# A fused two-block transformer in fp32: the first half of the mixer worked tile by tile, the zero stores moved to the last half block

## The chip, the cores and the metric

One core of a Trainium2 chip runs the whole program. The metric is the device time of one execution in microseconds (us), the median of the runs. The core has TensorE (PE in the rows; its weight loads are PEld), VectorE (DVE), ScalarE (ACT), GpSimd (POOL) and SyncE (SP); SP, ACT and POOL also issue DMA transfers, which run on the core's 16 DMA engines.

## The reference

512 tokens of width 1024, all float32. A first block of two layers, then a second block. What matters here is layer 0:

```python
mod = c_act @ ada_w[l] + ada_b[l]                  # 6 vectors of 1024: sh1, sc1, g1, sh2, sc2, g2
hn = modulate(rms_norm(h, norm_mix_g[l]), sh1, sc1)
mix = hgrn2_mixer(hn, ...)                         # q, f, v, g projections, scan over chunks of 16 tokens, w_out
h = h + g1[:, None, :] * mix
hn = modulate(rms_norm(h, norm_ffn_g[l]), sh2, sc2)
h = h + g2[:, None, :] * peer_ffn(hn, ...)
...
def peer_ffn(xn, w_q, subkeys, u, v):
    qr = xt @ w_q                                  # queries
    sc = einsum('thpd,hpnd->thpn', qr, subkeys)    # scores against 128 sub-keys, 4 heads x 2
    ...                                            # top 16 of each, top 16 of their sums: 64 experts a token
    hid = einsum('cd,ced->ce', xc, take(u, ec))    # 64 gathered rows of u for each token
    w = gc * gelu(hid)
    return einsum('ce,ced->cd', w, take(v, ec))    # and 64 of v
```

The scan carries its state from one tile of 128 tokens to the next. The second block has a short convolution, window attention and, at its end, 32 routed experts, whose tokens are scattered into a buffer in HBM of 3264 rows, cleared to zeros beforehand.

## The kernel before, in words

Four tiles of 128 tokens make two halves of 256 (`hf` 0 and 1). Layer 0 of half 0 is `first_pe`, `first_act` and `first_dve`, one Python generator for each engine, whose pieces between two `yield`s ("segments", counted by `s`) are laid out in step. The engines run their own instruction streams and wait on semaphores: `a_pe`, `a_act` and `a_dve` count finished steps by the names in `A_PE`, `A_ACT` and `A_DVE`.

**The order of the program.** Half 0 of the mixer runs alone. Then come four windows of two gathered tiles each (`rows_*`, `w` 0 to 3): POOL gathers rows of u and v, each gather 128 rows of 4 KB, into a ring of six pairs (regions `r2`, `r4`, `r3`); DVE makes the dot products with the u rows (`dots_dve`), PE sums the v rows (`sum_pe`), and the next half block of the network is laid between these steps. Window 0 holds half 1 of the mixer, window 3 half 0 of the second block. Half 1 of the second block runs alone behind the windows, and then the experts.

**Tail of half 0.** Behind the four projections and four levels of masked scores, PE does for both tiles together: the scan (L822 transposes, L831/L834 output, L840 new state), the head norms' sums (L849), the output projection (L188, four groups, each of one tile and 512 columns), the turning of the normed rows (L757), the query projection (L188 over 256 tokens), the turning of the keys (L1062), and the scores (L1069). ACT copies all scores (`sc3`), and only then does `route_dve` pick the experts of tile 0 (L369 to L429, about ten segments), after which POOL issues the first gather (L447).

**Modulation chunks.** The 28 chunks of `CHUNKS` are each 1024 x 512 of `ada_w` or `kv_ada_w`, 2 MB. Chunks 0 to 3 make sh1 and sc1 of layer 0, without which no projection begins. `mod_load` loads a chunk into `r5` or `r6` by turns; a chunk is multiplied with c either by PE (`mod_parts_pe` L667, then a copy L648 on DVE) where `BY_PE` says so, or by DVE (`mod_acc_dve` L651/L653, eight passes). `mod_sum_pe` (L678 or L681) adds over partitions, `mod_out_dve` (L693 to L706) finishes it. `MOD_SEG` says before which segment of half 0 this happens. SP issues chunks 0 and 1 and then the first two blocks of mixer weights; POOL (`mods_pool`) issues each later chunk j once chunk j-2 is done.

**Weights.** SP streams all weights through two slots (`stream`, `load_weights`): block i may be loaded when block i-2 has had its last use (`slot_free`, `A_LAST_USE`).

**Zero stores.** At the end of `mods_pool`, ahead of its first gather, POOL issues 26 stores of zeros (`zero_slots`) from `HOLE` into the experts' buffer `x_slots`.

## Time and profile before

| what | value |
|---|---|
| time of three runs | 3090.72, 3091.57, 3102.13 us; median 3091.57 |
| the profiled execution | 3102.22 us, span 3100.7 us, mean granted clock of TensorE 0.825 |
| busy, of the span | PE 71%, DVE 48%, ACT 15%, POOL 36% |
| moved by DMA | 992.03 MB, mean 320 GB/s |
| chain that ended last | PE 44%, DVE 15%, DMA 14%, issue 9%, POOL 4%, ACT 4% |
| half 0 of the mixer alone | 0 to 323.8 us (its last score matmul) |
| routing of tile 0 | 325.9 to 353.7 us |
| windows of gathers | 354 to 2206 us |
| half 1 of the second block | 2206 to about 2450 us, then the experts |

Busy shares are averages over these stages, which have different limits; a stage is read by what it waits for last. The profiled execution lies 10.65 us above the median, so a sum made on its rows is carried over as a share or a difference. In the rows a matmul in float32 counts as two instructions, and "x16" in a row of the PE are eight matmuls.

### The profile page before, as it was taken

Reading aid. Unit: us, or ns where it says so; the run is one execution under the profiler, and the core shown is the slowest. Engines: PE = TensorE matmul, PEld = TensorE weight load, DVE = VectorE, ACT = ScalarE, POOL = GpSimd, SP = SyncE. Lnnn points to the kernel's source line nnn. Section 1 sums busy time; section 2 is a strip of 40 time slices with the busy share of each in tenths; the row PEclk is TensorE's granted clock in tenths of the full one; section 3 lists DMA queues with packets and bytes.
Section 4 is the critical chain, followed back from the end, with each engine's and each line's share of the span. In section 5 each row is a group of like instructions: output and inputs, shape, how many; then the busy total and the mean of one; then the engine's idle time right before and its main releaser. Section 6 shows DMA issues by size and latency. Waiting matters only on the chain.

```text
span 3100.7 us, 28191 instructions
## 1 busy us (share of the span) xinstructions
PE 2191.7 (71%) x10377; PEld 1247.3 (40%) x10377; DVE 1491.4 (48%) x3207; ACT 470.5 (15%) x790; POOL 1126.9 (36%) x1278
## 2 busy tenths in 40 slices
PE   5998294786547596457886358568797588888873
PEld 3574273533325342325642136233576333232321
DVE  3867699644773425853425865661145212121112
ACT  1212111020102410102510101110222101010111
POOL 2111445565652655642555754455100111010001
PEclk8999697898768797658997678789898789898997
DMA  8984999899996999986999989989433579999994
GB/s 302 345 326 174 360 353 394 335 375 379 337 406 242 359 368 368 341 340 242 320 377 358 371 333 330 319 294 380 153 132 126 212 281 356 391 361 402 390 400 163
DMA packets 269877, 992.03 MB, mean 320 GB/s; under 512 B 26925, under 2 KB 33173, under 8 KB 257463
## 3 DMA queue, kind: packets, MB, share of 16 engines
q0 software_dynamic: 175056, 634.01, 54.2%
q1 hardware_dynamic: 89440, 350.26, 29.8%
q10 hardware_dynamic: 5256, 6.05, 0.6%
q8 instruction: 83, 1.36, 0.2%
q14 instruction: 42, 0.34, 0.0%
HBM read 961.62 MB, written 28.61 MB: 319 GB/s over the span
## 4 chain that ended last, share of the span: by engine, by line
PE 44%; DVE 15%; DMA 14%; another core or an unknown queue 9%; issue 9%; POOL 4%; ACT 4%; POOLq 0%; SPq 0%; DVEq 0%; ACTq 0%
PE psum L188 24%; DMA arena<-in_w_down_dram 7%; PE psum L2089 6%; POOL arena L447 4%; DVE arena L459 4%; PE psum L552 4%; PE psum L2103 3%; DMA arena<-in_peer_v_dram,arena 3%; DMA arena<-in_ada_w_dram 2%; DVE arena L1632 1%; PE psum L1412 1%; PE psum L1188 1%; DVE arena L653 1%; DMA arena<-in_hgrn_w_in_dram 1%
## 5 line engine op out<-in xcount | busy, mean ns | idle before, releaser
L188 PE MATMUL psum<-arena 128*128 128x256 f32 (+4 forms) x3656 | 1015.1, 435 | 175.1 <-issue 122.8
L188 PEld LDWEIGHTS psum<-arena 128*128 128x128 f32 x3656 | 710.9, 200 | 495.7 <-issue 373.2
L447 POOL DMA_INDIRECT arena<-in_peer_u_dram,arena x512 | 489.2, 955 | 475.1 <-DVE arena L459 221.9
L447 POOL DMA_INDIRECT arena<-in_peer_v_dram,arena x512 | 497.7, 972 | 393.0 <-PE psum L552 147.2
L459 DVE CUSTOM_DVE_ANT_0 arena<-arena,psum 128x1024 f32<-128x1024 f32 x512 | 592.6, 1216 | 75.0 <-DMA arena<-in_peer_u_dram,arena 51.6
L552 PE MATMUL psum<-arena 128*32 128x512 f32 x2048 | 327.7, 762 | 185.2 <-DMA arena<-in_peer_v_dram,arena 161.4
L2089 PE MATMUL psum<-arena 128*64 128x512 f32 x1088 | 268.8, 651 | 61.8 <-DMA arena<-in_w_down_dram 60.4
L552 PEld LDWEIGHTS psum<-arena 128*32 128x32 f32 x2048 | 69.1, 126 | 378.9 <-issue 377.1
L2136 DVE TENSOR_TENSOR arena<-arena,psum 64x512 f32<-64x512 f32 x34 | 23.5, 692 | 326.4 <-ACT arena L2117 326.4
L2089 PEld LDWEIGHTS psum<-arena 128*64 128x64 f32 x1088 | 82.9, 150 | 222.0 <-issue 220.0
L2150 POOL DMA_DIRECT2D arena<-x_slots x37 | 19.2, 519 | 397.7 <-DVE arena L2124 379.6
L2103 PE MATMUL psum<-arena 128*64 128x512 f32 x544 | 145.3, 683 | 17.6 <-DVE arena L2140 17.6
L2025 POOL DMA_INDIRECT x_slots<-arena x8 | 7.8, 972 | 274.2 <-DVEq L174 272.0
L653 DVE SCALAR_TENSOR_TENSOR arena<-arena 128x512 f32<-128x512 f32 x133 | 100.0, 752 | 4.7
L2117 ACT ACTIVATE arena<-psum 64x512 f32<-64x512 f32 x34 | 20.0, 589 | 510.2 <-PE psum L2089 510.2
L1632 DVE SCALAR_TENSOR_TENSOR arena<-arena 128x256 f32<-128x256 f32 x240 | 97.3, 479 | 0.0
L757 PE MATMUL psum<-arena 128*128 128x128 f32 x128 | 26.9, 397 | 98.1 <-DVE arena L948 55.6
L1188 PE MATMUL psum<-arena 128*128 128x256 f32 (+1 forms) x208 | 55.2, 434 | 52.1 <-DVE arena L1279 51.3
L2144 DVE COPY arena<-psum 128x512 f32<-128x512 f32 x34 | 23.5, 692 | 127.7 <-PE psum L2103 127.7
L2166 POOL DMA_DIRECT2D x_slots<-arena x68 | 36.9, 542 | 129.0 <-DVE arena L2144 127.5
L599 POOL DMA_DIRECT2D arena<-in_ada_w_dram x22 | 20.4, 929 | 168.2 <-DVE arena L653 97.7
L2103 PEld LDWEIGHTS psum<-arena 128*64 128x64 f32 x544 | 40.9, 156 | 96.6 <-issue 74.4
(328 smaller groups left out, 2011.4 us busy)
## 6 DMA issues: line engine op xcount, KB each, us to landing
arena<-in_w_gate_dram SPq DMA_DIRECT2D x32, 2048.0 KB, 24.3
arena<-in_w_up_dram SPq DMA_DIRECT2D x32, 2048.0 KB, 13.0
arena<-in_w_down_dram SPq DMA_DIRECT2D x32, 2048.0 KB, 18.6
arena<-in_ada_w_dram POOLq DMA_DIRECT2D x22, 2048.0 KB, 10.0
arena<-in_hgrn_w_in_dram SPq DMA_DIRECT2D x16, 2048.0 KB
arena<-in_w_in_dram SPq DMA_DIRECT2D x14, 2048.0 KB
arena<-in_peer_w_q_dram SPq DMA_DIRECT2D x8, 2048.0 KB
arena<-in_kv_w_dram SPq DMA_DIRECT2D x8, 2048.0 KB
```

The costliest lines, as they stand in the source:

```text
L188: last = pe.matmul(o, lhsT=lhs(k), rhs=rhs(k), start=start and k == 0, stop=stop and k == n - 1)
L447: pool.indirect_dma_start(RING(n, k), None, (U_TAB, V_TAB)[v], bass.IndirectOffsetOnAxis(ap=at, axis=0))\
L459: last = dve.tensor_tensor_reduce(out=row, in0=row, in1=bank(XB0, 0, D), scale=1.0, scalar=0.0, op0=ALU.mult, op1=ALU.add, accum_out=par_s ...
L552: last = pe.matmul(bank(ACC + half, 0, 512, parts=(32 * g, 32)), lhsT=mem("t", D + (s // 4 % 2) * 512 + (g * GR + s % 4) * 32, 32), rhs=RI ...
L653: ins = dve.scalar_tensor_tensor(MOD_ACC(j), MOD_W(j)[:, k, :], C_COL(k), MOD_ACC(j), ALU.mult, ALU.add)
L757: last = pe.transpose(bank(b, (k % 2) * 256 + i * P, P), src(i, k), ident)
L1188: last = pe.matmul(bank(ZB(h), o + w - min(w, wm), min(w, wm)), lhsT=mem("negtri" if m == n else "negones", 0, P), rhs=AW(hf, h, om, wm), ...
L1412: last = pe.matmul(bank(b, p * 256, 256, parts=(64 * a, 64)), lhsT=wslot(i)[:, k, a * 256 + (2 * b + p) * 64:a * 256 + (2 * b + p) * 64 + 64],
L1632: ins = dve.scalar_tensor_tensor(Y2(hf, c), CV(c, 256 * hf + i, 256), CCOL(c, i), Y2(hf, c), ALU.mult, ALU.add)
L2089: last = pe.matmul(bank(2, 0, FF, parts=half(m)), lhsT=XBT[:, k, :], rhs=EW(e, m)[:, k, :], start=k == 0, stop=k == KD - 1, skip_group_che ...
L2103: last = pe.matmul(bank(4, 0, 512, parts=half(n)), lhsT=HT[:, k, :], rhs=EW(e, 2)[:, k, n * 512:(n + 1) * 512], start=k == 0, stop=k == NF ...
L2166: pool.dma_start(y_slots[bass.ds(g * SLOTS, SLOTS), m * 512:(m + 1) * 512], mem("w1", 0, D // 2, parts=half(m)))\
```

## The change

**Tile by tile.** In half 0, `lead_pe`, `lead_act` and `lead_dve` take the place of the tail from the scan on. Each step is done for tile 0 (128 tokens) and then for tile 1, and tile 0 goes through output, norm, queries and scores while tile 1 follows. `route_dve(0)` waits for `sc1`, the scores of tile 0 alone; the first gather also waits for PE's `sc3`, since the ring lies on regions that half 0 uses.

**Keys and query weights.** The sub-keys are loaded by ACT's queue at the start and turned before anything else (`keys_pe`, `keys_act`). Of the query weights the first 512 columns go to `r4` (`QUERY_W`), the others to a slot.

**Chunks.** Chunks 0 to 3 have four buffers and are all issued by SP at the start, ahead of the mixer weights. `MOD_SEG` is spread otherwise, chunks 26 and 27 go by PE, and the last pieces of chunks 25 to 27 stand between the segments of the routing (`BESIDE_ROUTE`).

**Zero stores.** They are issued by POOL behind its last gather, once all eight gathered tiles are added (`acc_used`), from a region that it clears there; `dispatch_pool` waits for them.

```diff
@@ load_weights
+                if i == marks["peer_q00"]:
+                    sp.wait_ge(sem("a_pe"), a_pe(0, "dl11"))
+                    sp.dma_start(QUERY_W, w_cols(A["peer_w_q"][0], 0)).then_inc(sem("query_w"), 16)
@@ setup_sp
-            for j in range(2):
+            for j in range(FIRST_CHUNKS):          # 4
                 mod_load(sp, j)
@@ setup_act
             x_half(0)
+            act.dma_start(KEYS_RAW, KEYS0).then_inc(sem("keys_in"), 16)
@@ route_dve
-                dve.wait_ge(sem("a_act"), a_act(t >= 2, "sc3"))
+                dve.wait_ge(sem("a_act"), a_act(t >= 2, "sc3" if t else "sc1"))
@@ gather_pool
+            if (v, t, s) == (0, 0, 0):
+                pool.wait_ge(sem("a_pe"), a_pe(0, "sc3"))
@@ chunks
-        MOD_SEG = {...} | dict(zip((17, 18, 20, 21, 22, 24, 25, 27, 29, 31, 32), range(17, NCHUNK)))
-        BY_PE = [j < 4 or 17 <= j < 22 for j in range(NCHUNK)]
+        MOD_SEG = {...} | dict(zip((17, 18, 19, 20, 21, 24, 28, 30, 31, 32, 33), range(17, NCHUNK)))
+        BY_PE = [j < 4 or 17 <= j < 22 or j >= 26 for j in range(NCHUNK)]
+        BESIDE_ROUTE = {1: (25, 1), 2: (26, 0), 4: (26, 1), 6: (27, 0), 8: (27, 1)}
+        MOD_W = lambda j: mem(("r5", "r6", "r3", "r2")[j] if j < FIRST_CHUNKS else ("r5", "r6")[j % 2], 0, KD, 512)
@@ mods_pool
-            for j in range(2, NCHUNK + 6):
+            for j in range(FIRST_CHUNKS, NCHUNK + 6):
-                    pool.wait_ge(sem("mod_acc"), j - 1)
+                    pool.wait_ge(sem("mod_acc"), j - 1 if j >= FIRST_CHUNKS + 2 else j - FIRST_CHUNKS + 1)
-            for i in range(N_CLEAR):
-                zero_slots(pool, i)
@@ A_LAST_USE of half 0
-        [..., "o1", "o3", "pq1", "pq3", "kt1"]
+        [..., "o1", "o3", "pq3"]
@@ lead_pe (new; called by first_pe for half 0 behind the levels)
+            scan(0); squares(0, 0); scan(1)
+            out(0, 0, 0)                  # tile 0, columns 0 to 511, bank 0
+            squares(1, 2)
+            out(0, 1, 1); out(1, 0, 2)
+            turned(0)                     # waits xn0
+            out(1, 1, 1)
+            queries(0, 0); queries(0, 1); scores(0)
+            turned(1)                     # waits xn1
+            queries(1, 0); queries(1, 1); scores(1)
@@ rows_dve
+            for n, _ in enumerate(route_dve(dve, 0, link)):
+                if n in BESIDE_ROUTE:
+                    j, out_of = BESIDE_ROUTE[n]
+                    (mod_out_dve if out_of else mod_acc_dve)(dve, j, link)
@@ rows_pool, behind the last window
+            pool.wait_ge(sem("acc_used"), TILES)
+            link(pool.memset(ZEROS, 0.0))
+            for i in range(N_CLEAR):
+                zero_slots(pool, i)
@@ dispatch_pool
             pool.wait_ge(sem("slots"), 1)
+            pool.wait_ge(sem("cleared"), 16 * N_CLEAR)
```

The `lead_pe` lines above are its calls in their order, without the waits and yields between them. Three places show how the instructions stand now. The first is PE in half 0 from the output projection on, before: L188 is a projection, L678 the sum of a chunk, L757 the turning of both tiles.

```order
L188 MATMUL psum<-arena 128x512 x8
L678 MATMUL psum<-arena 1x512
L757 MATMUL psum<-arena 128x128 x16
L188 MATMUL psum<-arena 128x256 x16
L678 MATMUL psum<-arena 1x512
L188 MATMUL psum<-arena 128x256 x32
L678 MATMUL psum<-arena 1x512
L188 MATMUL psum<-arena 128x256 x16
L678 MATMUL psum<-arena 1x512
L1062 MATMUL psum<-arena 128x128 x8
L1069 MATMUL psum<-arena 128x128 x16
```

The same place in the changed kernel, from the first query matmuls of tile 0 on: L196 is a projection, L947 the scores of one tile, L929 the turning of tile 1, L689 the sum of a chunk, L678 the parts of chunks 26 and 27.

```order
L196 MATMUL psum<-arena 128x128 x32
L947 MATMUL psum<-arena 128x128 x8
L689 MATMUL psum<-arena 1x512
L678 MATMUL psum<-arena 32x512 x8
L929 MATMUL psum<-arena 128x128 x8
L689 MATMUL psum<-arena 1x512
L678 MATMUL psum<-arena 32x512 x8
L196 MATMUL psum<-arena 128x128 x64
L689 MATMUL psum<-arena 1x512
L947 MATMUL psum<-arena 128x128 x8
L689 MATMUL psum<-arena 1x512
```

The scores of tile 0 now stand ahead of half of the query work, and the sum of chunk 26 (the second L689 from the end) stands behind all of it. The second place is DVE in the changed kernel, from the state of tile 1 to the last chunk ahead of the routing: L1271/L1272 add an output group to h, L662/L664 are a chunk, L1277/L1278 the normed tile.

```order
L1271 TENSOR_TENSOR psum<-psum,arena 128x512
L1272 TENSOR_TENSOR arena<-arena,psum 128x512
L1271 TENSOR_TENSOR psum<-psum,arena 128x512
L1272 TENSOR_TENSOR arena<-arena,psum 128x512
L662 TENSOR_SCALAR arena<-arena 128x512
L664 SCALAR_TENSOR_TENSOR arena<-arena 128x512 x7
L704 SCALAR_TENSOR_TENSOR arena<-psum,arena 1x512
L1276 RECIPROCAL arena<-arena 128x1
L1277 SCALAR_TENSOR_TENSOR arena<-arena 128x1024
L1278 TENSOR_TENSOR arena<-arena 128x1024
L662 TENSOR_SCALAR arena<-arena 128x512
L664 SCALAR_TENSOR_TENSOR arena<-arena 128x512 x7
```

Between the last sum into tile 1 and its norm there is now a whole chunk (24), and a second (25) behind it; before, tile 1's norm followed at once. The third place is DVE within the routing of tile 0 in the changed kernel: L391 finds indices, L704 finishes chunk 26 and L396 forms the candidate sums.

```order
L659 COPY arena<-psum 128x512
L387 MAX arena<-arena 128x8 x8
L391 MAX_INDEX arena<-arena 128x8 x8
L704 SCALAR_TENSOR_TENSOR arena<-psum,arena 1x512
L396 TENSOR_TENSOR arena<-arena 128x1024
L398 CAST arena<-arena 128x128
```

Before, L391's and L396's counterparts (L383, L388) followed one another; now the end of chunk 26 is between them.

## Rows read from the trace of the kernel before

**Rows 1.** The page: DMA share in tenths, 40 slices of 77.5 us.

```profile
DMA  8984999899996999986999989989433579999994
```

**Rows 2.** DVE in order of time: start, length, line, tiles, idle before.

```profile
325.89 1.65 DVE L369 MAX8 arena<-arena 128x8 f32<-128x128 f32 x8 [7.15 <-ACT arena L1096]
...
353.88 1.22 DVE L477 COPY psum<-arena 128x1024 f32<-128x1024 f32 x1
367.63 1.22 DVE L459 CUSTOM_DVE_ANT_0 arena<-arena,psum 128x1024 f32<-128x1024 f32 x1 [12.53 <-DMA arena<-in_peer_u_dram,arena]
```

**Rows 3.** The chain of waits: a piece in the routing of tile 0.

```profile
335.90 1.24 DVE arena L388
```

**Rows 4.** POOL in order of time: zero stores and first gather.

```profile
319.52 13.73 POOL L1930 DMA_DIRECT2D x_slots<-arena  x26
354.25 1.02 POOL L447 DMA_INDIRECT arena<-in_peer_u_dram,arena  x1 [21.01 <-DVE arena L429]
```

**Rows 5.** Windows: busy by engine, PEclk, DMA share, GB/s.

```profile
320.00:340.00 20.00, 3.76 (x32) 3.56 (x32) 13.87 (x78) 3.35 (x5) 13.24 (x26) 0.68 1.03 394
...
360.00:380.00 20.00, 0.67 (x3) 0.67 (x4) 11.86 (x25) 0.00 (x0) 14.36 (x16) 0.50 1.02 406
400.00:450.00 50.00, 46.02 (x201) 38.77 (x200) 49.59 (x126) 6.54 (x9) 25.33 (x27) 0.97 1.00 383
```

**Rows 6.** PE in order of time: the parts of chunks 2 and 3.

```profile
34.28 3.23 PE L667 MATMUL psum<-arena 128*32 128x512 f32 x16 [9.99 <-DMA arena<-in_ada_w_dram]
...
42.50 3.64 PE L667 MATMUL psum<-arena 128*32 128x512 f32 x16 [4.00 <-DMA arena<-in_ada_w_dram]
```

**Rows 7.** POOL in order of time: loads of chunks 2 and 3.

```profile
20.73 1.12 POOL L599 DMA_DIRECT2D arena<-in_ada_w_dram  x1 [9.58 <-DVE arena L648]
24.37 0.92 POOL L599 DMA_DIRECT2D arena<-in_ada_w_dram  x1 [2.52 <-DVE arena L648]
```

**Rows 8.** PE in order of time, scan to scores of half 0.

```profile
217.14 1.09 PE L822 MATMUL psum<-arena 128*128 128x128 f32 x8 [0.94 <-DVE arena L1006]
...
222.53 1.92 PE L667 MATMUL psum<-arena 128*32 128x512 f32 x16
224.38 1.09 PE L822 MATMUL psum<-arena 128*128 128x128 f32 x8
...
230.76 1.02 PE L678 MATMUL psum<-arena 128*1 128x512 f32 x2
...
242.63 16.93 PE L188 MATMUL psum<-arena 128*128 128x512 f32 x32 [5.77 <-issue]
...
282.47 3.68 PE L757 MATMUL psum<-arena 128*128 128x128 f32 x16 [5.93 <-DVE arena L1113]
286.89 7.17 PE L188 MATMUL psum<-arena 128*128 128x256 f32 x32 [0.75 <-ACT arena L1083]
...
319.92 3.84 PE L1069 MATMUL psum<-arena 128*128 128x128 f32 x32 [0.86 <-ACT arena L1092]
```

**Rows 9.** DVE in order of time: a chunk's passes, a pass over a tile.

```profile
254.66 5.48 DVE L653 SCALAR_TENSOR_TENSOR arena<-arena 128x512 f32<-128x512 f32 x7
...
277.21 1.28 DVE L1112 SCALAR_TENSOR_TENSOR arena<-arena 128x1024 f32<-128x1024 f32 x1
```

**Rows 10.** ACT in order of time: the square root of a tile's norm.

```profile
269.07 1.06 ACT L1041 ACTIVATE arena<-arena 128x1024 f32<-128x1024 f32 x1 [28.94 <-DVE arena L1104]
...
271.53 0.29 ACT L1043 ACTIVATE arena<-arena 128x1 f32<-128x1 f32 x1
```

**Rows 11.** The page, part 6: loads of chunks, us to landing.

```profile
arena<-in_ada_w_dram POOLq DMA_DIRECT2D x22, 2048.0 KB, 10.0
```

**Rows 12.** SP queue in order of time: the query weights.

```profile
259.59 16.40 SPq L140 DMA_DIRECT2D arena<-in_peer_w_q_dram  x2
```

**Rows 13.** Windows: the 34 us behind the last gathered tile.

```profile
2206.00:2240.00 34.00, 24.99 (x115) 22.06 (x116) 5.88 (x10) 11.42 (x23) 0.00 (x0) 0.85 0.18 62
```

**Rows 14.** PE in order of time: first projection behind them.

```profile
2218.69 27.89 PE L188 MATMUL psum<-arena 128*128 128x256 f32 x128 [0.93 <-ACT arena L1535]
```

More of the change, by code:

```diff
@@ new lines, in keys_pe, with keys_act @@
+        def keys_pe(pe):
+            pe.wait_ge(sem("keys_in"), 16)
+            for a in range(2):
+                for j in range(4):
+                    last = pe.transpose(bank(2 + a, j * P, P), KEYS_RAW[:, 4 * a + j, :], ident)
+                last.then_inc(sem("a_pe"), 1)
+        def keys_act(act):
+            for a in range(2):
+                act.wait_ge(sem("a_pe"), a_pe(0, f"kt{a}"))
+                act.activation(SKTA(4 * a, 512), bank(2 + a), ACT.Copy).then_inc(sem("a_act"), 1)
@@ L932, in first_act, with lead_act, scan, norm @@
                                 lambda k, n=256: ab("F", hf, k * 256, n), lambda g, n: ab("C", hf, g * 256, n))
+        def lead_act(act, on_pe, on_dve, on_self, did):
+            def scan(i):
+                for a in range(2):
+                    on_pe(f"k2t{i}{a}")
+                    did(act.activation(ab("KN", 0, i * D + a * 512, 512), bank(2 + a), ACT.Copy))
+                for a in range(2):
+                    on_pe(f"om{i}{a}")
+                    did(act.activation(ab("C", 0, i * D + a * 512, 512), bank(a), ACT.Copy))
+                on_self(f"oe{i}1")
+                did(act.activation(ONSQ(i, 0, D), ab("C", 0, i * D, D), ACT.Square))
+            def norm(i, b):
+                for a in range(2):
+                    on_pe(f"ss{i}{a}")
+                    did(act.activation(ONSQ(i, a), bank(b + a), ACT.Ln, scale=1.0 / P, bias=col(COL_EPS)))
+                for a in range(2):
+                    on_self(f"lo{i}{a}")
+                    did(act.activation(ONSQ(i, a), ONSQ(i, a), ACT.Exp, scale=-0.5))
+            def turned(i):
+                for a in range(2):
+                    on_pe(f"turn_2_{2 * i + a}")
+                    did(act.activation(ab("F", 0, a * D + i * P, (256, 4), P), bank((3, 0)[a], 0, 4, P), ACT.Copy))
+            def queries(i):
+                for a in range(2):
+                    on_pe(f"pq{2 * i + a}")
+                    did(act.activation(ab("C", 0, a * D + i * P, (256, 4), P), bank((3, 0)[a], 0, 4, P), ACT.Copy))
+            def scores(i):
+                for a in range(2):
+                    on_pe(f"sc{2 * i + a}")
+                    did(act.activation(mem("r1", i * D + a * 512, 512), bank((2, 1)[a]), ACT.Copy))
+            scan(0)
+            norm(0, 0)
+            yield
+            scan(1)
+            norm(1, 2)
+            yield
+            on_dve("h0")
+            rms_act(act, 0, ab("Q", 0, 0, D), "sq2_0", on_self, did)
+            turned(0)
+            yield
+            on_dve("h1")
+            rms_act(act, 1, ab("Q", 0, D, D), "sq2_1", on_self, did)
+            queries(0)
+            scores(0)
+            yield
+            turned(1)
+            queries(1)
+            act.wait_ge(sem("mod_out"), GAINS_USED)
+            scores(1)
+            yield
         def first_dve(dve, hf, link):
```

256 lines of the change are left out of this document (215 added, 41 removed).

## The prediction

> **What bounds the kernel now.** I read the page first, then each engine in order of time for the first 380 us, then the windows where the zero stores lie and where they will lie. The page's DMA line shows three stages: 8s and 9s from slice 5 to slice 28, which are the windows of gathers, then 4, 3, 3, 5, which is the last half block, then 9s for the experts [rows 1]. In none of them is a time fixed by anything but the step before, so what the start loses or gains is carried to the end unless a later stage absorbs it.
>
> The start has a long serial piece. PE, DVE and ACT finish half 0; then DVE alone routes tile 0, from 325.89 to 353.88 [rows 2], with one inner mark at 335.90, where the sums of candidates begin [rows 3]. POOL issues the zero stores at 319.52 and the first gather at 354.25 [rows 4]. The gather's rows don't come at once: DVE's first dot product starts at 367.63 after 12.53 us of waiting for them [rows 2], and the DMA share is 1.03 at 320 to 340 and still 1.02 at 360 to 380 [rows 5]. The reason is arithmetic: 25 stores of 512 KB and one of 256 KB are 13.4 MB, with two weight blocks of 2.1 MB behind them 17.6 MB; at the row's 394 to 406 GB/s that is 44 us from 319.5, thus to about 363. Once the dots run, DVE is busy 49.59 of 50 us at 400 to 450 [rows 5], so the first stretch of window 0 is paced by DVE, and an earlier first dot shifts it whole.
>
> **The change part by part.** I count to two marks, first gather and first dot.
>
> *Front, four chunks first.* Chunk 2 was issued at 20.73 and PE got it at 34.28; chunk 3 was issued at 24.37 and PE got it at 42.50 [rows 6, 7]. Issued at 3 us they could come sooner, but the engines are already full: 14.7 MB (x, four chunks, two blocks of weights) had to pass by 42.5. Chunk 2 took 13.55 us, which is 5.3 MB at 390 GB/s, of which it was 2.1: POOL's queue got about half beside SP's. Now POOL issues chunks 4 and 5 as soon as chunks 0 and 1 are copied, at the same 20.7 and 24.4, and these take the same half. SP has some 4.2 MB of chunks 2 and 3 left at 22.7 us (2 us for the start of POOL's queue, 1.3 us lost to the 0.5 MB of keys); at half of 390 this ends at 22.7 + 20.9 = 43.6, against 42.50. The front costs about 1 us. Bounds: SP's queue served alone would bring chunk 3 at 33.4, a gain of 9; loss at most 3.
>
> The Trainium skill, "DMA: Bandwidth & Descriptors", section on queues, rings and completion order, says that each DMA engine goes round robin between queue rows with work, packet by packet. By that rule too the early issue buys nothing here, and the trace agrees with 40% to 50% for POOL's queue; if it were wrong, the 9 us above would be the result.
>
> *Levels.* The parts of chunk 21 (1.92, [rows 8]) now stand ahead of the scan. PE would start it at 217.14 + 1.9 + 0.5 for a later level + 1 from the front = 220.
>
> *PE from scan to scores.* Before: 217.14 to 323.76, 106.6 us [rows 8], with idle time of 5.77 (it waits for both tiles' gating), 5.93 (for both norms), and 16 matmuls at the lower clock, 16.93 instead of 14.2. After, at durations of the same rows: scan of tile 0 4.65, scan of tile 1 6.4 (224.38 to 230.76); 4 output groups of 7.1; query projections 128 matmuls of 128 columns at 0.24 (3.84 for 16 [rows 8]) = 30.8, where before 64 of 256 columns at 0.44 took 28.4; turning 3.7, scores 3.8, head norms 1.8, seven sums of chunks 6.7, parts of chunks 26 and 27 3.8. Sum 90. Waits: the norm of tile 0 is ready 0.6 after PE is (its three DVE passes take 2.7, [rows 9] for one, and square to root 2.8 [rows 10]). Chunk 27 is the larger: POOL may load it only when DVE has finished chunk 25. DVE does 24 (6.0, [rows 9]) ahead of tile 1's norm and 25 behind it, ending 65 us after the scan's start; with 10.0 to landing [rows 11] it comes at 75, while PE is ready at 70.5, so 4.5. Total 95: last score matmul at 220 + 95 = 315, against 323.8.
>
> *Query weights.* SP issues the block to `r4` behind the wait for o1, since the wait for its slot stands ahead of it in the loop; o1 is done 37 us after the scan's start, PE wants it at 46.7. Before, at the same event, the pair took 259.59 to 276 to issue and was never waited for [rows 12]. At 10.0 to landing [rows 11] it is 0.3 late; I take 0. Behind it in SP's queue are the other query block, wanted at 55, and a block of half 1.
>
> *Routing of tile 0.* It may start when tile 0's scores are copied, 65.5, in fact at 67.3 behind chunk 24's end. But it is not free to run: chunk 26 must be finished (L704) between L391 and L396, and PE sums it only behind all queries of tile 1, at 93.3. DVE reaches this place at 67.3 + 10.0 (325.89 to 335.90) + 2.1 for chunks 25 and 26 = 79.4 and stands 13.9 us. Then 0.7, the rest of the routing 17.85 (335.90 to 353.75), and 1.4 for chunk 27: 113.2. POOL adds 0.3. First gather at 220 + 113.5 = 333.6, 20.6 earlier than 354.25. Thus only about half of the 40 us by which the scores of tile 0 come earlier (325.9 to 285.5) reaches the gather. PE's scores are done at 315, so the new wait for `sc3` costs nothing; if it ever came last, 20 us of cover would have to be gone.
>
> *First dot.* Its pair is issued by 333.6 + 2.2. Before, it took 13.4 from first issue to first dot with the queue full. Empty, the pair's 1.05 MB need at least 2.6 at 400 GB/s; half of a 2 MB load's 10.0 us is 5; I take 6. First dot at 341.8, against 367.63: 25.8 earlier. Bounds 20.6 (nothing from the zeros) and 29.
>
> *Zero stores in the last half block.* 13.4 MB are 34 us at 394 GB/s, and the 34 us behind 2206 have a DMA share of 0.18 [rows 13]. PE eats a block of weights in 14 us (27.89 for two [rows 14]), and two are loaded. The third is issued when the first is used up, at about 2232, and would get half the rate beside the zeros: 10.7 + 2, in by 2245, when the second ends. I take 0; bounds 0 and 8. With that cover gone it would be up to 34.
>
> **Sum.** 25.8 earlier on the profiled execution's own 3102.22, thus 3076.4 or 0.83% less. On the median of 3091.57 the same share is 25.7: 3065.9, rounded 3066. 0.5% (15.5 us) is about what a measurement of this kernel can tell from no change.
>
> **The rivals.**
> 1. *Front at its full worth.* SP's queue ahead of POOL's brings chunk 3 9 us sooner and all shifts: 3056. For it: SP's DMAs are all queued by 5 us. Against: chunk 2's 13.55 us. 12%.
> 2. *Loads come late in the tail.* Between 37 and 65 us after the scan starts, SP queues the query blocks and one of half 1, POOL chunks 25 to 27. If query block 1 and chunk 27 take 8 to 9 us more each, PE slips by 17 and with it the sum of chunk 26: gain 9, 3083. For it: the chunk loads' spread (chunk 3 took 18 us); against: PE's only stretch here without idle is short of traffic. 12%.
> 3. *The gain is absorbed in window 0.* Its DVE pace gives way to PE and gathers after about 100 us; if the next half's steps set the pace, only the earlier scores of tile 1 (9 us) count: 3083. Against: those steps too hang on DVE's dots in one order. 11%.
> 4. *Slower.* The zeros collide with the last half block: each weight block waits its turn and all 34 us appear; 25.8 - 34 is 8 slower, 3100; with rival 2 also true more. It decides from 26 us of new PE waits for weights behind 2206. Against: a share of 0.18 there. 7%.
> 5. *The routing gains nothing*, as the wait at chunk 26 is longer still (PE late by 20): only the 5 to 8 us from the empty queue: 3084. 6%.
>
> **How the numbers follow.** My forecast has 52%, with its own range 3056 to 3077. Faster by over 0.5% (under 3076.1): nearly all of it (50) and rival 1 (12), and parts of 2 and 3 (6): 0.68. Within 0.5%: 0.24. Slower: rival 4 and surprises, 0.08. The range runs from rival 1, with a little more, to rivals 2, 3 and 5: 3052 to 3087.
>
> **What would show it.** Chunk 3's parts on PE at 43 to 44 (34: rival 1). The scan at 219 to 221, last scores at 313 to 317. A wait of about 14 us on DVE for PE ahead of L396, and the first L457 at 331 to 336. First dot 6 to 9 us behind it. Behind the last gathered tile, no wait of PE for weights, and DMA share near 1 for 34 us. The prediction falls if chunk 27 or the query weights keep PE waiting for over 10 us, or if window 0 is longer than before by over 10 us from its first dot.

## The result, and the profile after

The kernel before takes 3098.45 us (median of 18 executions, 3080.03 to 3109.09), the changed kernel 3078.9 us (median of 18, 3069.36 to 3088.26). The ratio is 0.9945, with a 95% interval of 0.9929 to 0.9962: 17 us faster by the ratio (the two medians lie 19.55 us apart). The profiled execution went from 3102.22 to 3079.18 us, its span from 3100.7 to 3077.6. On another chip, where the changed kernel was measured once more (last table of the experiments), the ratio is 0.9887 (0.9863 to 0.9911), 33 us faster. The two intervals don't overlap, and the kernel before has no profile on that chip, so the size of the gain isn't the same everywhere, and where the other 16 us lie is open. What follows explains the gain of the profiled executions in the first table.

The order of reading is that of the prediction. First the page's DMA line, 40 slices of the span, beside [rows 1]:

```profile
DMA  8985699999987999987999989989744579989995
```

The 9s of the gathers now begin one slice later (slice 5 has a 6, where the stores stood before), and the last half block, slices 29 to 32, has 7, 4, 4, 5 where it had 4, 3, 3, 5. That is the move of the zero stores seen from afar.

Second, DVE in order of time around the routing of tile 0, the answer to [rows 2]:

```profile
284.22 1.65 DVE L377 MAX8 arena<-arena 128x8 f32<-128x128 f32 x8
291.82 0.68 DVE L704 SCALAR_TENSOR_TENSOR arena<-psum,arena 1x512 f32<-1x512 f32 x1 [3.74 <-issue]
309.20 0.68 DVE L704 SCALAR_TENSOR_TENSOR arena<-psum,arena 1x512 f32<-1x512 f32 x1 [9.17 <-issue]
310.03 1.22 DVE L396 TENSOR_TENSOR arena<-arena 128x1024 f32<-128x1024 f32 x1
...
329.44 1.22 DVE L487 COPY psum<-arena 128x1024 f32<-128x1024 f32 x1
336.77 1.22 DVE L469 CUSTOM_DVE_ANT_0 arena<-arena,psum 128x1024 f32<-128x1024 f32 x1 [6.11 <-DMA arena<-in_peer_u_dram,arena]
```

The routing starts 41.7 us earlier (284.22 against 325.89), but the first dot product only 30.9 us (336.77 against 367.63). Between them stand two waits of 3.74 and 9.17 us at L704, the line that adds a chunk's sum. The wait is put down to "issue" here; PE's row tells whose it was. PE in order of time, same stretch:

```profile
285.19 3.64 PE L678 MATMUL psum<-arena 128*32 128x512 f32 x16 [3.27 <-DMA arena<-in_ada_w_dram]
288.76 1.97 PE L929 MATMUL psum<-arena 128*128 128x128 f32 x8
290.66 1.05 PE L689 MATMUL psum<-arena 128*1 128x512 f32 x2
291.75 1.92 PE L678 MATMUL psum<-arena 128*32 128x512 f32 x16
293.60 14.56 PE L196 MATMUL psum<-arena 128*128 128x128 f32 x128
308.09 1.02 PE L689 MATMUL psum<-arena 128*1 128x512 f32 x2
309.04 2.05 PE L947 MATMUL psum<-arena 128*128 128x128 f32 x16
```

PE's sums at L689 end at 291.71 and 309.11, and DVE goes on 0.1 us behind each. The second one stands behind all 14.56 us of tile 1's query projections.

Third, POOL in order of time, and the windows (busy time of PE, PEld, DVE, ACT, POOL, then PEclk, DMA share, GB/s), beside [rows 4, 5]:

```profile
283.06 0.94 POOL L612 DMA_DIRECT2D arena<-in_ada_w_dram  x1 [4.65 <-DVE arena L664]
...
329.80 1.02 POOL L457 DMA_INDIRECT arena<-in_peer_u_dram,arena  x1 [3.88 <-DVE arena L437]
```

```profile
280.00:290.00 10.00, 6.73 (x33) 2.69 (x32) 7.76 (x30) 1.28 (x3) 1.92 (x3) 0.70 0.92 335
290.00:300.00 10.00, 9.97 (x79) 7.23 (x78) 7.93 (x43) 1.11 (x2) 0.49 (x1) 0.96 0.07 24
300.00:310.00 10.00, 10.00 (x84) 9.02 (x83) 0.72 (x2) 1.20 (x2) 0.00 (x0) 1.00 0.08 19
...
320.00:330.00 10.00, 0.00 (x0) 0.00 (x0) 9.52 (x14) 2.89 (x5) 0.68 (x2) 0.50 0.00 0
...
2178.00:2212.00 34.00, 26.36 (x121) 23.28 (x122) 5.40 (x9) 11.18 (x23) 14.86 (x27) 0.85 0.95 358
```

The first gather is 24.5 us earlier (329.80 against 354.25). Ahead of it the DMA engines now have little to do from 292 on: shares of 0.07, 0.08 and 0.00. Where they had 0.18 behind the last gathered tile [rows 13] they have 0.95.

Last, PE behind that tile, the answer to [rows 14]:

```profile
2189.31 27.89 PE L196 MATMUL psum<-arena 128*128 128x256 f32 x128 [0.93 <-ACT arena L1799]
2222.39 15.86 PE L1676 MATMUL psum<-arena 128*64 128x256 f32 x128 [5.19 <-DMA arena<-in_w_in_dram]
```

PE waits 5.19 us for the third block of weights, and the following line takes 15.86 us instead of 14.04 before: the granted clock is 0.71 from 2217.0 to 2222.4, while PE stands, and 0.88 in the 15.6 us behind. So the last half block gives back 7.1 us of the 30.9.

Every profile of this kernel can be cut at three marks: first dot (DVE), end of the last gathered tile (DVE, L574), first scatter of the dispatch (POOL, L2300; the lines are the changed kernel's). All that follows is told in the pieces between them, in us of the profiled execution; "rest" is what comes behind the first scatter. The last column puts the first and third piece alone on the kernel before, and leaves the other two as they were: 1 + (difference) / 3100.7.

| kernel | first dot | windows | last half block | rest | ratio measured | by 1st and 3rd |
|---|---|---|---|---|---|---|
| before | 367.6 | 1838.3 | 256.6 | 638.2 | 1 | 1 |
| changed | 336.8 | 1839.8 | 263.7 | 637.4 | 0.9945 | 0.9923 |
| zeros_alone | 362.5 | 1827.4 | 262.5 | 636.0 | 1.0012 | 1.0003 |
| tiles_alone | 372.6 | 1824.6 | 256.6 | 634.7 | 1.0010 | 1.0016 |
| sums_late | 324.0 | 1829.7 | 260.8 | 639.1 | 0.9869 | 0.9873 |
| zeros_paced | 338.7 | 1824.3 | 264.1 | 637.8 | 0.9918 | 0.9931 |
| two_buffers | 341.0 | 1826.5 | 263.7 | 640.9 | 0.9959 | 0.9937 |
| late_and_paced | 325.3 | 1833.3 | 265.8 | 636.8 | 0.9892 | 0.9893 |
| zeros_in_gap | 336.9 | 1819.0 | 256.8 | 637.2 | 0.9924 | 0.9902 |

The measured ratios are of medians on several chips, the pieces of one execution each. The profiled execution of the kernel before lies 3.8 us above its median of 18, and the windows differ by up to 21 us from one execution to another. So a difference of some 0.002 between the last two columns says nothing. The expectations below also name a time for the profiled execution; four of them missed it although the pieces came as expected, since the windows were 10 to 21 us shorter than in the kernel before or the changed one: zeros_alone had 3090.35 us (expected 3098 to 3106), tiles_alone 3090.03 (3101 to 3110), zeros_in_gap 3051.39 (3072), and sums_late 3055.15 (3068 to 3070).

### The profile page after: what moved, and what is told of

Same layout as the page of the kernel before. It is cut to its first block, busy times and chain, and to the rows that moved or that the text cites. A ratio compares the mean times of both kernels' runs of the same rounds, so it can differ in the third digit from the quotient of the medians.

```text
span 3077.6 us, 28513 instructions
## 1 busy us (share of the span) xinstructions
PE 2179.0 (71%) x10537; PEld 1247.5 (41%) x10537; DVE 1482.4 (48%) x3202; ACT 473.6 (15%) x786; POOL 1121.4 (36%) x1276
## 4 chain that ended last, share of the span: by engine, by line
PE 46%; DMA 15%; issue 13%; DVE 13%; another core or an unknown queue 4%; POOL 4%; ACT 3%; SPq 1%; POOLq 0%; DVEq 0%; ACTq 0%
PE psum L196 26%; DMA arena<-in_w_down_dram 8%; PE psum L2364 6%; POOL arena L457 4%; PE psum L562 3%; PE psum L2378 3%; DVE arena L469 3%; DMA arena<-in_peer_v_dram,arena 3%; DMA arena<-in_hgrn_w_in_dram 2%; PE psum L1676 1%; DVE arena L1896 1%; PE psum L1452 1%; DVE arena L664 1%; DMA arena<-in_ada_w_dram 1%
## 5 line engine op out<-in xcount | busy, mean ns | idle before, releaser
L196 PE MATMUL psum<-arena 128*128 128x256 f32 (+3 forms) x3784 | 1016.4, 425 | 169.8 <-issue 118.1
L196 PEld LDWEIGHTS psum<-arena 128*128 128x128 f32 x3784 | 716.1, 200 | 486.3 <-issue 362.3
L562 PE MATMUL psum<-arena 128*32 128x512 f32 x2048 | 319.9, 747 | 188.9 <-DMA arena<-in_peer_v_dram,arena 158.1
L2364 PE MATMUL psum<-arena 128*64 128x512 f32 x1088 | 269.8, 653 | 72.9 <-DMA arena<-in_w_down_dram 70.4
L2411 DVE TENSOR_TENSOR arena<-arena,psum 64x512 f32<-64x512 f32 x34 | 23.5, 692 | 338.7 <-ACT arena L2392 338.7
L2378 PE MATMUL psum<-arena 128*64 128x512 f32 x544 | 132.1, 630 | 17.6 <-DVE arena L2415 17.6
L2300 POOL DMA_INDIRECT x_slots<-arena x8 | 7.8, 974 | 249.1 <-DVEq L182 247.0
L664 DVE SCALAR_TENSOR_TENSOR arena<-arena 128x512 f32<-128x512 f32 x119 | 89.5, 752 | 4.2
L1452 PEld LDWEIGHTS psum<-arena 128*128 128x128 f32 x208 | 44.8, 252 | 62.7 <-DVE arena L1543 54.2
## 6 DMA issues: line engine op xcount, KB each, us to landing
arena<-in_w_up_dram SPq DMA_DIRECT2D x32, 2048.0 KB, 13.3
```

What stands on the lines that cost most here:

```text
L196: last = pe.matmul(o, lhsT=lhs(k), rhs=rhs(k), start=start and k == 0, stop=stop and k == n - 1)
L562: last = pe.matmul(bank(ACC + half, 0, 512, parts=(32 * g, 32)), lhsT=mem("t", D + (s // 4 % 2) * 512 + (g * GR + s % 4) * 32, 32), rhs=RI ...
L664: ins = dve.scalar_tensor_tensor(MOD_ACC(j), MOD_W(j)[:, k, :], C_COL(k), MOD_ACC(j), ALU.mult, ALU.add)
L1452: last = pe.matmul(bank(ZB(h), o + w - min(w, wm), min(w, wm)), lhsT=mem("negtri" if m == n else "negones", 0, P), rhs=AW(hf, h, om, wm), ...
L2364: last = pe.matmul(bank(2, 0, FF, parts=half(m)), lhsT=XBT[:, k, :], rhs=EW(e, m)[:, k, :], start=k == 0, stop=k == KD - 1, skip_group_che ...
L2378: last = pe.matmul(bank(4, 0, 512, parts=half(n)), lhsT=HT[:, k, :], rhs=EW(e, 2)[:, k, n * 512:(n + 1) * 512], start=k == 0, stop=k == NF ...
```

## The experiments

### zeros_alone and tiles_alone: each half of the change by itself

zeros_alone is the kernel before with the stores moved from the end of `mods_pool` to the end of `rows_pool`:

```diff
-            for i in range(N_CLEAR):
-                zero_slots(pool, i)
...
+            pool.wait_ge(sem("acc_used"), TILES)
+            link(pool.memset(ZEROS, 0.0))
+            for i in range(N_CLEAR):
+                zero_slots(pool, i)
```

> The kernel before, with one edit of the change: the zero stores stand behind the last gather instead of ahead of the first. First theory (two chains ended together): in the kernel before, tile 0's routing on DVE ends at 353.88 and POOL has issued the zero stores by 354.25, so taking the stores away frees nothing for the first gather; it still issues at 353 to 354. Only the landing behind the stores goes: the first dot comes 7 us behind the gather instead of 13.4, at about 361 (6 to 7 us earlier), and the last half block gives 7 us back to the stores. Sum: profiled 3102, between 3098 and 3106. Second theory (the stores held the first gather): the gather comes some 30 us earlier, and the time falls by 20 us or more, to about 3080.

Measured: ratio 1.0012 (0.999 to 1.0035). The first gather comes at 355.92, behind DVE's L428 and not a microsecond earlier; the first dot at 362.50; the last half block takes 262.5 us, 5.9 more. The first theory holds in each piece: the 5.1 us won at the first dot are paid back at the end. (The scan started 2.9 us later in this execution, at 220.07 against 217.14, so the first dot gained rather more than 5.1.)

tiles_alone is the changed kernel with the stores put back at the end of `mods_pool`, out of a region of 512 words that is free there (`ZEROS`, read twice for a row):

```diff
+            for i in range(N_CLEAR):
+                zero_slots(pool, i)
...
-            for i in range(N_CLEAR):
-                zero_slots(pool, i)
```

> The changed kernel, with the zero stores put back ahead of the first gather (their zeros in 512 words of another region, each row read twice from them). First theory (two chains ended together): POOL's last row store is at 325.44, the 26 stores take 34.7 us to issue as in the kernel before, so the first gather issues at 360 and the first dot comes at 367 to 374, no earlier than the 367.63 of the kernel before; the last half block is 7 us shorter than in the changed kernel. Sum: 3101 to 3110, so no gain from the tile by tile half. Second theory (the tile by tile half gives the gain by itself): 3072, the changed kernel less the 7 us of the last half block.

Measured: ratio 1.0010 (0.998 to 1.004). Here is DVE, and then POOL:

```profile
331.25 1.22 DVE L488 COPY psum<-arena 128x1024 f32<-128x1024 f32 x1
372.58 1.22 DVE L470 CUSTOM_DVE_ANT_0 arena<-arena,psum 128x1024 f32<-128x1024 f32 x1 [40.12 <-DMA arena<-in_peer_u_dram,arena]
```

```profile
327.73 18.26 POOL L2203 DMA_DIRECT2D x_slots<-arena  x26
346.29 1.04 POOL L458 DMA_INDIRECT arena<-in_peer_u_dram,arena  x1 [0.30 <-issue]
```

DVE is ready at 332.5 and stands 40.12 us, since the gather is queued behind 13.4 MB of zeros. The issue took 18.26 us, not the 34.7 that I expected, so the gather was issued at 346.29 rather than 360; the landing decides, and that came inside 367 to 374.

What follows: the kernel before had **two chains that ended within some 5 us of each other**, the routing of tile 0 and the drain of the stores. Neither edit alone gave anything (both intervals hold 1); the gain is in both together.

One thing makes tiles_alone look worse than tile by tile work as such. The stores stand on POOL behind the row store of the last chunk, and the change finishes that chunk inside the routing. So they are issued 8.2 us later than in the kernel before (327.73 against 319.52), and they drain at 351 GB/s (330 to 340) where the kernel before has 394 (320 to 340). By an estimate from these rows (8.2 us, and 13.4 MB at either rate, 4.2 us) the first dot would come near 360 without that: some 7 us earlier than before, still far from 336.8. The drain stays the limit either way, and zeros_in_gap below shows it from the other side.

### sums_late: the wait on DVE inside the routing

```diff
-        BESIDE_ROUTE = {1: (25, 1), 2: (26, 0), 4: (26, 1), 6: (27, 0), 8: (27, 1)}
+        BESIDE_ROUTE = {1: (26, 0), 2: (25, 1), 4: (27, 0), 8: (26, 1), 9: (27, 1)}
```

> The changed kernel, with the order of the five pieces that stand between tile 0's routing steps changed: both copies of the last two chunks first, the pieces that wait for PE's sums last. DVE waits 3.74 us and 9.17 us in the changed kernel for these sums. First theory (that wait is on the chain): the waits shrink from 12.9 to about 1 to 2 us, the first gather issues at 318 to 320 instead of 329.80, the first dot comes at 325 to 327 instead of 336.77, and the profiled time falls by 9 to 11 us, to 3068 to 3070. Second theory (the first window's later part has another bound, such as the next half's mixer or the gathers' own rate): the first dot comes 10 us earlier and the end of tile 0 does not, and the time is within 3 us of 3079.

Measured: ratio 0.9869 (0.982 to 0.9919). DVE in order of time:

```profile
310.48 0.68 DVE L704 SCALAR_TENSOR_TENSOR arena<-psum,arena 1x512 f32<-1x512 f32 x1
315.44 0.67 DVE L704 SCALAR_TENSOR_TENSOR arena<-psum,arena 1x512 f32<-1x512 f32 x1
...
323.95 1.22 DVE L469 CUSTOM_DVE_ANT_0 arena<-arena,psum 128x1024 f32<-128x1024 f32 x1 [6.46 <-DMA arena<-in_peer_u_dram,arena]
```

Both L704 now run without a wait, the first gather is at 317.24 and the first dot 12.8 us earlier. So the two waits were on the chain, 1 : 1. But the span fell by 24.0 us, twice what the first theory allows. The table shows where: 10.1 us came in the windows and 2.9 in the last half block, where nothing was edited, against 1.7 us lost in the rest. That had to be settled (below).

### zeros_paced: spread the stores over the last half block

What the last half block takes without the burst is read from tiles_alone (256.6) and zeros_in_gap (256.8). A kernel that leaves the stores out altogether (no_zeros, expected 7 us faster) has no time: rows of the experts' buffer would hold undefined values. zeros_paced keeps the stores there and spreads them.

```diff
             for i in range(N_CLEAR):
+                pool.wait_ge(sem("c_pe"), c_pe(1, C_PE[1][8 + i]))
                 zero_slots(pool, i)
```

> The changed kernel, its 26 zero stores still in the last half block but each held until PE has finished one more step of it, from the third projection on, instead of all being issued at the block's start. First theory (the burst of stores holds up the weights that the first projections wait for): PE's wait of 5.19 us at the first w_in line is gone, the stretch from the end of the last window to the first scatter of the dispatch falls from 263.7 us to 257, and the profiled time is 3072. Second theory (any place in the last half block costs the same, since its weights are late throughout): the stretch stays at 262 to 264 us and the wait appears further down.

Measured: ratio 0.9918 (0.9891 to 0.9945), but the last half block takes 264.1 us, as before the edit. PE in order of time:

```profile
2204.78 12.90 PE L1676 MATMUL psum<-arena 128*64 128x256 f32 x118
2217.61 7.29 PE L196 MATMUL psum<-arena 128*128 128x256 f32 x48
...
2229.81 5.41 PE L196 MATMUL psum<-arena 128*128 128x256 f32 x16 [3.31 <-DMA arena<-in_w_in_dram]
```

The wait at L1676 is gone and one of 3.31 us stands at the next block of weights, the first that is loaded beside a store. Of the two theories the second fits: SP loads a block when an earlier one is used up, so each comes just in time, and a mean DMA share of 0.4 there (0.40 in zeros_in_gap from 2240 to 2413, without any store) is no room for another transfer. It holds for the stretch in which the weights are loaded; split_16_10 below finds room for 10 stores ahead of them. The 3.31 us and the slower matmuls behind them are not all of the 7.5 us by which the stretch is longer than before; the rest wasn't traced. The ratio is no proof to the contrary: 0.9918 comes from windows of 1824.3 us.

### two_buffers: undo the four first chunk buffers

```diff
-        FIRST_CHUNKS = 4
+        FIRST_CHUNKS = 2
```

> The changed kernel with two first chunk buffers instead of four, the third and fourth chunk loaded by POOL as before. First theory (the whole first half of the mixer is bound by the bytes that it loads, not by when the first chunks come): the first projection moves back by about 3 us to 54 to 55, but the scan still starts at 216 to 218, and the first dot comes within 1.5 us of 336.8; time within 2 us of 3079. Second theory (the four buffers are worth their lead at the projections): the first dot comes 3 us or more later, 3082 or above.

Measured: ratio 0.9959 (0.9934 to 0.9984), first dot at 341.0. PE in order of time, first this kernel, then the changed kernel, the answer to [rows 6]:

```profile
18.98 1.94 PE L998 MATMUL psum<-arena 128*128 128x128 f32 x8 [13.89 <-DMA arena<-in_peer_subkeys_dram]
39.37 3.63 PE L678 MATMUL psum<-arena 128*32 128x512 f32 x16 [11.11 <-DMA arena<-in_ada_w_dram]
44.73 1.93 PE L678 MATMUL psum<-arena 128*32 128x512 f32 x16 [0.75 <-DMA arena<-in_ada_w_dram]
```

```profile
18.77 1.94 PE L998 MATMUL psum<-arena 128*128 128x128 f32 x8 [13.83 <-DMA arena<-in_peer_subkeys_dram]
20.64 5.54 PE L678 MATMUL psum<-arena 128*32 128x512 f32 x32
28.50 1.92 PE L678 MATMUL psum<-arena 128*32 128x512 f32 x16 [0.45 <-DMA arena<-in_ada_w_dram]
36.97 3.64 PE L678 MATMUL psum<-arena 128*32 128x512 f32 x16 [5.56 <-DMA arena<-in_ada_w_dram]
51.85 1.62 PE L196 MATMUL psum<-arena 128*128 128x256 f32 x3 [4.22 <-DMA arena<-in_hgrn_w_in_dram]
```

Chunk 3's parts stand at 44.73 without the buffers and at 36.97 with them. The scan of tile 0 starts at 221.45 without; in the six profiles of the first table that have them it starts at 216.25 to 218.88. So they are worth some 3 to 5 us at the scan beside early keys. What the keys cost by themselves isn't shown: the two kernels with neither (before, zeros_alone) start the scan at 217.14 and 220.07, but without the 1.92 us of chunk 21's parts ahead of it. My first theory, that the start is bound by bytes alone, expected the scan at 216 to 218 and falls; it was wrong too in the first projection, which moved back by 1.1 us (51.85 to 52.99) and not by 3. The second theory is right in the first dot, 4.2 us later, and not in the time (3073.58, expected 3082 or above; the windows were 13.3 us shorter). The 4.2 us are small against the interval of the ratio, and that row, not the ratio, carries the reading.

### zeros_in_gap: the stores where the DMA engines are idle

```diff
             for j in range(FIRST_CHUNKS, NCHUNK + 6):
+                if j == NCHUNK + 1:
+                    for i in range(N_CLEAR):
+                        zero_slots(pool, i)
...
-            for i in range(N_CLEAR):
-                zero_slots(pool, i)
```

As in tiles_alone, each row is read as two halves from 512 words of zeros.

> The changed kernel, with the zero stores issued behind chunk 27's load and its row store, at about 287, into the stretch from 292 to 330 in which the DMA engines are nearly idle in the changed kernel. First theory (the stores cost only what they collide with): they are issued by 305 and drained by 330, the first gather still issues at 329.8 and the first dot still comes at about 337, the last stretch falls to 257 us, time 3072. Second theory (they hold up the last chunk's transfer or the rows' stores on POOL's queue and so tile 0's routing, or run into the gather): first dot at 342 or later, time 3078 or above.

Measured: ratio 0.9924 (0.9901 to 0.9947), first dot at 336.9, last half block 256.8 us. POOL and the windows:

```profile
286.74 18.26 POOL L2204 DMA_DIRECT2D x_slots<-arena  x26
...
330.23 1.01 POOL L458 DMA_INDIRECT arena<-in_peer_u_dram,arena  x1 [3.88 <-DVE arena L438]
```

```profile
300.00:310.00 10.00, 10.00 (x83) 9.02 (x83) 0.37 (x1) 1.19 (x2) 5.52 (x9) 1.00 1.02 384
310.00:320.00 10.00, 3.38 (x16) 1.41 (x14) 9.72 (x36) 2.73 (x4) 0.50 (x1) 0.73 1.02 376
320.00:330.00 10.00, 0.00 (x0) 0.00 (x0) 9.51 (x17) 0.00 (x0) 0.48 (x1) 0.50 1.03 405
```

The engines are full at 384 to 405 GB/s through the stretch that was empty, and nothing is later for it by more than 0.5 us. The same 13.4 MB cost 36 us at the first dot of tiles_alone, 7 in the last half block, and nothing here.

### late_and_paced, and the question of the windows

> Both edits: the sums for the last two chunks at the end of tile 0's routing, as in the run before, and the zero stores spread over the last half block. The first run with the late sums had its first dot 12.8 us earlier than the changed kernel and ended 24.0 us earlier. First theory (the two edits are at different places and add, and 11 us of those 24 were chance of one execution in the second window): first dot at 324, the last stretch 257 us, time 3079 - 13 - 6 = 3060, 3048 if the second window keeps its 11 us. Second theory (the windows return an earlier start with interest): 3048 or less in every execution.

The edits are the two diffs above. Measured: ratio 0.9892 (0.9859 to 0.9925), first dot at 325.3, windows 1833.3, last half block 265.8 (I had expected 257; as in zeros_paced, the spread stores give nothing). The late sums' gain at the first dot is there again (11.5 us), of the windows' 10.1 us only 6.5. Against zeros_paced, measured in the same runs and different by the late sums alone, the median falls by 12.8 us (3060.35 to 3047.56), as much as the first dot. But the six executions lie between 3042.26 and 3062.71, on both sides of the second theory's 3048. This speaks for the first theory without deciding; three more runs were made on another chip:

> The changed kernel once more, without an edit, for a second profile of it. In its first profile the four windows of gathers took 1839.7 us from the first dot to the end of the last tile; in the profiles of seven other kernels that differ only ahead of the windows or behind them it was 1819.0 to 1838.3. First theory (that spread is chance of one execution, the gathers' transfers running at slightly different rates): this profile has another value of that range, probably some 10 us less, with the first dot within 2 us of 336.8 and the last stretch at 263.7. Second theory (the start of this kernel makes its windows long): 1837 to 1842 again.

> The kernel with the late sums once more, without an edit. Its first profile gained 12.8 us at the first dot, 10 in the windows and 2.9 in the last stretch against the first profile of the changed kernel. First theory (only the first of these is the edit's): the first dot at 323 to 326, the windows anywhere from 1819 to 1840, and its median 10 to 16 us below that of the changed kernel in the same runs. Second theory (the windows return more): the windows at 1826 to 1831 again and the median 20 us or more below.

> The late sums, with 16 of the 26 zero stores issued at about 287 into the gap of the DMA engines and the other 10 at the start of the last half block, where the kernel before shows a DMA share of 0.00 for 20 us. First theory (a store costs only what it collides with): the 16 are drained by 315, ahead of the first gather at 317, so the first dot stays at 324 to 325; the 10 are drained by 2175 or so, ahead of SP's next weight loads, so the last stretch is 257 instead of 261 to 266; the ratio to the kernel before is 0.9869 less 0.0020, about 0.985. Second theory (POOL's queue or the row stores behind the zeros are the limit): the first dot at 328 or later or the last stretch at 260 or more, and the ratio is 0.987 or above.

split_16_10 adds to the late sums, with `IN_GAP = 16`:

```diff
+                if j == NCHUNK + 1:
+                    for i in range(IN_GAP):
+                        zero_slots(pool, i)
...
-            for i in range(N_CLEAR):
+            for i in range(IN_GAP, N_CLEAR):
                 zero_slots(pool, i)
```

| kernel, on the other chip | first dot | windows | last half block | rest | median | ratio to before |
|---|---|---|---|---|---|---|
| before | | | | | 2940.46 | 1 |
| changed_again | 338.1 | 1675.1 | 262.6 | 630.9 | 2907.4 | 0.9887 (0.9863 to 0.9911) |
| sums_late_again | 324.9 | 1671.0 | 263.5 | 641.5 | 2901.53 | 0.9875 (0.9852 to 0.9897) |
| split_16_10 | 325.0 | 1671.7 | 255.3 | 635.3 | 2899.18 | 0.9857 (0.9831 to 0.9884) |

The first dot and the last half block are what they were on the first chips, within 3 us; the windows are some 160 us shorter, and now equal within about 4 us. So the late sums are worth 13 us at the first dot, and most of the rest of the first 24 was the windows' own spread, not the edit's. My size for changed_again's windows (10 us less than 1839.7) was off by far, for the reason told in the last section. The medians of the late sums and of the changed kernel differ by 5.9 us here, less than the 10 to 16 expected; their intervals overlap, and the one piece that went against it is the rest (641.5 against 630.9), which lies outside all edits. So 13 us are shown at the first dot and, in one set of runs, in the median; here the medians show no more than half of it.

split_16_10 has both gains at once. Its 10 late stores are issued from 1999.27, ahead of the weights; PE shows no wait at the line that had 5.19:

```profile
2009.46 27.89 PE L196 MATMUL psum<-arena 128*128 128x256 f32 x128 [0.93 <-ACT arena L1805]
2037.28 14.04 PE L1682 MATMUL psum<-arena 128*64 128x256 f32 x128
```

Its ratio of 0.9857 is the lowest of all; against sums_late_again the order is likely and not proven by the medians, while the piece is plain (263.5 to 255.3).

## Why the prediction was right, and where it was not

The forecast was 3066 us or 0.83% less; measured were 0.55% less, on the profiled execution 23.0 us where 25.8 were forecast. The direction, the place and the mechanism held, and the size held in part by luck: two errors of opposite sign nearly cancel (below), and another chip shows 1.13%. By its steps:

- **Front: 1 us later. Wrong in sign, by some 4 us.** Chunk 3's parts came at 36.97, not 43.6, the first projection at 51.85 instead of 54.51 before, now waiting for its weights, and the scan at 216.54, not 220 (the terms of that sum give 220.5). Less the 2.4 us for chunk 21 and a level, the front is 3.0 us earlier. The step that failed is that POOL issues chunks 4 and 5 "at the same 20.7 and 24.4": the early keys, which I priced at 1.3 us of transfer, arrive only at 18.77 and PE turns them first, so chunk 0's parts start at 20.64, DVE copies them at 26.26, and POOL issues at 27.25 and 28.93. The 2 MB loads of POOL that I had put beside SP's third and fourth chunk thus were not there yet. That two_buffers brings the parts back to 44.73 shows the buffers' part in it; how much of it is due to POOL's late issue alone isn't shown.
- **PE from scan to scores: 95 us. Measured 94.6** (216.54 to 311.09). But the waits lie elsewhere: 3.27 us for chunk 26, none for chunk 27, for which 4.5 had been taken. So near a hit is partly luck.
- **Routing waits 13.9 us at L396. Measured 9.17 there and 3.74 at the sum of chunk 25, together 12.9.** I had given the latter nothing: its sum on PE stands behind chunk 26's late load. sums_late shows that both count in full.
- **First gather 333.6, first dot 341.8. Measured 329.80 and 336.77.** The 3.8 us are nearly all the front's; the latency was 6.97 where I took 8.2.
- **The zeros cost 0 in the last half block, bounds 0 and 8. Measured 7.1.** The mechanism was in the text (the third block gets half the rate beside the stores) and its size wrong: "10.7 + 2, in by 2245". That block was issued at 2203.42 and PE went on with it at 2222.39, 19.0 us later. Transfers of the changed kernel from 2203 to 2222 by queue (packets, MB, share), q0 being POOL's and q1 SP's:

```profile
q0 software_dynamic: 1287, 4.64, 66.6%
q1 hardware_dynamic: 1522, 2.59, 36.0%
```

The packets are shared almost evenly, but those of the stores carry 3.6 KB and those of the weights 1.7 KB, so the weights get 36% of the bytes: at the window's 381 GB/s in all, 2.1 MB take 15 us and not 10.7. The Trainium skill's rule that the prediction quoted ("DMA: Bandwidth & Descriptors", section on queues, rings and completion order: round robin packet by packet) fits this row; I had turned it into half of the bytes. Rival 4 was this mechanism at nearly five times its price.
- **The gain survives window 0.** Yes: 30.9 us at the first dot, 29.4 at the end of the last tile.
- **The sum.** Two errors of opposite sign, +5.0 (front, wait and latency) and -7.1 (zeros), made 23.8 of 25.8; the windows were 1.5 us longer and the rest 0.8 shorter, which leads to the 23.0 of the profiled executions.

What the prediction did not see is that the two halves would give nothing apart. It named both chains and summed their gains to 25.8, without saying what either would give if the other stayed. Its lower bound of "20.6 (nothing from the zeros)" takes the routing's gain as free of the drain; in tiles_alone, with the stores still ahead, the first dot is 5 us later than in the kernel before.

## What to carry to other kernels

When two chains end at nearly the same time, price a change by cutting each alone and then both, in thought: each alone is worth little, and the gain of the pair belongs to neither. Put a bulk transfer where the DMA share is near 0.00 in a window of 10 us, not where it is 0.2 to 0.4 on average: with loads that are issued just in time, an average share is no slack, and pacing the transfer moves the wait without shortening the stretch. Count a shared engine by packets, and then ask how large each side's packets are. What is slipped in between the steps of a critical piece should be what is ready by then, since the engine stands at it otherwise, as DVE did for 12.9 us; moving five such entries by a few places gave 13 us at the first dot. And when a gain measures twice as much on another chip, as here, name the chip with it, and compare kernels only within one set of runs.

## What the runs showed of the hardware

**PE stands without a known cause in the windows, in some sets of runs.** PE in order of time, in the second window, for the changed kernel and then for the same kernel on the other chip:

```profile
832.87 0.58 PE L196 MATMUL psum<-arena 128*128 128x256 f32 x1 [2.22 <-issue]
835.70 0.58 PE L196 MATMUL psum<-arena 128*128 128x256 f32 x1 [2.24 <-issue]
838.50 0.58 PE L196 MATMUL psum<-arena 128*128 128x256 f32 x1 [2.22 <-issue]
```

```profile
779.68 27.89 PE L196 MATMUL psum<-arena 128*128 128x256 f32 x128 [0.73 <-ACT arena L1484]
813.88 30.70 PE L196 MATMUL psum<-arena 128*128 128x512 f32 x64 [6.31 <-DMA arena<-in_kv_w_dram]
```

One matmul each 2.8 us, with nothing in the profile that it waits for, against 128 in a row. From 480 to 1990 us such idle time of PE adds up to 162 to 252 us in the nine profiles of the first table, and to 0 to 3 us in the three of the second. That is as large as the 160 us between their windows, and it differs by up to 90 us between executions whose windows differ by up to 21. The cause stays open. One candidate is the loading of instructions. The Trainium skill, "Runtime: NRT & Kernel Launch", section on instruction fetch mechanics, says that each engine refills its instruction memory through a DMA queue of its own and that this is mostly hidden. Here the trace speaks against it. The page has this line, the same for the changed kernel on both chips:

```profile
q8 instruction: 84, 1.38, 0.2%
```

That is 84 packets of 16 KB whether PE stands for 245 us or not at all, their median is 1.06 us long on the first chip and 1.08 on the other, and none of them lies between 810 and 860 us, the stretch of the rows above. From 824 to 843.4 us, in which seven matmuls stand alone, the two instruction queues (q8 and q14) moved one packet of 8 KB.

**SP's issue stands at the third 2 MB load.** In the changed kernel the issue of the four first chunks lasts from 2.91 to 19.41, and the first weights of the mixer are issued behind it:

```profile
2.91 1.04 SPq L612 DMA_DIRECT2D arena<-in_ada_w_dram  x2
4.00 6.01 SPq L612 DMA_DIRECT2D arena<-in_ada_w_dram  x1
10.05 9.36 SPq L612 DMA_DIRECT2D arena<-in_ada_w_dram  x1
19.46 5.16 SPq L148 DMA_DIRECT2D arena<-in_hgrn_w_in_dram  x1
```

In two_buffers, too, the first two loads take 1.05 us to issue; the third and fourth, there weight blocks, take 6.10 and 9.24. The prediction's rival 1 took all of SP's DMAs as queued by 5 us.

**The price of issuing the stores** was 13.73 us for 26 in the kernel before, 14.10 in the changed one, and 18.26 where each row is read as two halves, so it follows the form of the transfer. split_16_10 has both forms in one execution: 0.71 us for a store with its rows halved (11.32 for 16) and 0.57 for a whole one (5.70 for 10).
